# Heads of 64 columns worked by twos on TensorE, in a two-layer block with a second block behind it

## The chip, the cores and the metric

One core of one Trainium2 chip. The metric is the device time of one execution of the whole program in microseconds (us); a figure for a kernel is the median over its runs. A profile is of one execution, which has its own time.

## The reference, cut to what matters

512 tokens of width 1024 go through a first block of two layers and a second block of one. The part that the change touches is attention with heads of 64 columns, in three forms, and the norms:

```python
# first block, per layer: 'a' (8 heads, one shared key and value head, top-k mask)
rel = relu(einsum('thd,sd->ths', qi, ki))              # 4 index heads of 64
iscore = einsum('ths,th->ts', rel, wi); sel = top_k(where(causal, iscore, -inf), 128)
o_a = softmax(mask_sel(qa @ ka.T / 8)) @ va            # 8 heads of 64
# 'b' (4 heads, two score maps each, values of 128 columns)
o_b = (softmax(q1 @ k1.T / 8) - lam * softmax(q2 @ k2.T / 8)) @ vb
h = h + (sigmoid(gate_a) * (o_a @ w_a) + sigmoid(gate_b) * (norm(o_b) @ w_b)) @ w_out
h = h + (gelu(conv(rms_norm(h) @ w_up_gate)) * conv(rms_norm(h) @ w_up_val)) @ w_down
h = h + sigmoid(rms_norm(h) @ w_ple_gate) * (p @ w_ple_proj)
# second block: 'c' (8 heads of 64, own keys and values, bias by distance), a recurrence
# over 8 heads, 32 experts of which each token uses 2, layer norms in place of rms norms
```

## The kernel before, in words

Everything is fp32. Large weights are cut into two rounded parts: ScalarE copies a block to wh (L1805, a "cut"), VectorE subtracts for wl (L1274), and each product is three matmuls (hi x hi, lo x hi, hi x lo; L873 to L875, L1036 to L1038). Weight blocks come by DMA into a ring of three. The activations lie transposed, hT[:, k, :] for k of 8 parts by 512 tokens. All five engines have their program in a fixed order written out by hand; they meet through semaphores, and eight PSUM banks are given out beforehand by a plan (`bank.plan`): `opened(key)` on TensorE waits until the bank's previous use is emptied, `filled` and `emptied` count.

Attention (`attention`, L1061 for TensorE, L1474 for VectorE, ScalarE's likewise) walks a list of jobs; m is 0 and 1 for the two layers (16 jobs "b", then 32 jobs "a") and 2 for the second block (32 jobs "c"). A job is (kind, ti, h): 128 queries ti, head h, keys up to 128(ti+1), outer loop over ti, inner over h. Step s does on TensorE: scores of job s (L1079, banks 2 to 4 in turn); some pieces of a gate projection (`fill` says how many: 4, 2 or 1; L1036 to L1038); the transposes of job s-2's probabilities (L1087, banks 5 and 6); the values of job s-3 (L1109, bank 7, all heads of one ti). Head h has rows 64*(h%2) of the query and key tiles, and its values go to partitions 64*(h%2) of bank 7. VectorE does in step s a cut if one is due (`cuts_at`), then scale, mask and row minimum of job s (L1496), then the normalization of job s-1 (L1541, L1544). ScalarE does the cut, the exponential of job s (L1907), the copy of job s-2's transposed probabilities to PT[(s-2)%2] (L1913), and every fourth step of "a" (second of "b") the sigmoid of a finished gate (L1893). "b" jobs have two score maps (e=0, 1, on rows 0 to 63 and 64 to 127) and their output gets a norm of its own (L898 sums, L905 spread).

The projections (`first_projections`, 21 steps) hold the index scores: twelve (three ti by four heads), two in each of steps 5 to 10, one at the step's start and one after the rotation (L1027, bank 6), all in bank 7 (L958). ScalarE takes the relu of each (L1857), the second one as the last thing of its step, behind the square of the step's tile (L1872). VectorE adds them up and later seeks the top 128 by repeated max8 (L1440, L1443).

A norm (r = 0 to 7) is: squares of the eight parts on ScalarE (L1814), seven additions to ACC on VectorE (L1283, L1290), column sums over ACC on TensorE (L898: 4 matmuls, 8 passes), scaling, root and reciprocal on four columns (L1295, L1818, L1297), a spread back over the partitions (L905), then u and its two rounded parts, one k after the other (L1307, L1822, L1315). Norms 6 and 7 are layer norms and sum hT itself. The FFN's first up tile waits for each k of it; the second up tile follows whole. `spread_heads` (L914) and the recurrence's products (L2262) are not changed; they are matmuls of 64 output columns that lie in the two halves in turn.

## Time and profile before

| | |
|---|---|
| median of 3 runs | 3105.61 us (3098.68 to 3106.81) |
| profiled execution, own time | 3098.97 us |
| its span, mean granted TensorE clock | 3097.5 us, 0.942 |
| TensorE matmul busy | 2842.3 us, 92% |
| VectorE busy | 1674.8 us, 54% |
| ScalarE busy | 1230.0 us, 40% |
| HBM | 110 GB/s over the span |

The profiled execution is 1.5 us longer than its span, and 6.6 us shorter than the median. A matmul's row begins where its first column enters; its end is modelled and reaches over the start of the next, so the distance of two starts is what a matmul costs the engine.

### The profile page before, as it was taken

To read this page: it belongs to the slowest core of one execution; us is meant where nothing else is said; L and a number is where in the kernel's file an instruction comes from. 1 tells how busy PE (TensorE), PEld (TensorE's weight loads), DVE (VectorE), ACT (ScalarE), POOL (GpSimd) and SP (SyncE) were. 2 spreads that over 40 slices of the span, in tenths; PEclk is the share of its full clock that TensorE was granted. 3 is DMA by queue.
4 is the path that set the end of the run, shared out by engine and by line. 5 is a ranking of instruction groups with operands and counts; after the bars stand their busy time and mean duration, and the time that the engine had idled before them with its cause. 6 is when DMAs were issued, how large, how long until landed. Compare 5 with 4: busy or idle time off the path is not lost.

```text
span 3097.5 us, 36057 instructions
## 1 busy us (share of the span) xinstructions
PE 2842.3 (92%) x14676; PEld 2102.9 (68%) x14676; DVE 1674.8 (54%) x2758; ACT 1230.0 (40%) x1793; POOL 119.5 (4%) x101
## 2 busy tenths in 40 slices
PE   6989999999999998999999998998989889679986
PEld 5766677888877776667788875856667658344445
DVE  4596445545445487445646455344433525477767
ACT  2217643423343216642424233244222322267665
POOL 0010000000000010000000000000000000022210
PEclk9999999999999899999999998989989889789998
DMA  3111222222222111223222221302111023379992
GB/s 116 65 55 67 73 106 89 96 95 95 92 85 69 57 69 62 75 80 118 82 95 96 95 82 68 124 24 77 42 44 52 35 90 135 151 260 392 372 347 95
DMA packets 64137, 334.90 MB, mean 108 GB/s; under 512 B 9568, under 2 KB 10336, under 8 KB 31072
## 3 DMA queue, kind: packets, MB, share of 16 engines
q1 hardware_dynamic: 58848, 324.14, 29.0%
q0 software_dynamic: 5120, 8.40, 0.9%
q8 instruction: 118, 1.93, 0.3%
q14 instruction: 51, 0.42, 0.0%
HBM read 312.58 MB, written 28.31 MB: 110 GB/s over the span
## 4 chain that ended last, share of the span: by engine, by line
PE 77%; DVE 12%; ACT 5%; DMA 3%; issue 2%; SPq 0%; POOL 0%; POOLq 0%; DVEq 0%; ACTq 0%
PE bank L873 14%; PE bank L875 14%; PE bank L874 14%; PE bank L1036 3%; PE bank L1079 2%; PE bank L1109 2%; PE bank L1038 2%; PE bank L1037 2%; PE bank L2931 2%; PE bank L2212 2%; ACT wh L1805 1%; DVE wl L1274 1%; PE bank L2917 1%; DMA arena<-in_WE 1%; PE bank L2918 1%
## 5 line engine op out<-in xcount | busy, mean ns | idle before, releaser
L873 PE MATMUL bank<-XH,wh 128*128 128x512 f32 x1344 | 542.8, 404 | 21.0 <-DVE XL L1315 16.9
L874 PE MATMUL bank<-XL,wh 128*128 128x512 f32 x1344 | 531.8, 396 | 0.0
L875 PE MATMUL bank<-XH,wl 128*128 128x512 f32 x1344 | 531.4, 395 | 0.0
L1274 DVE TENSOR_TENSOR wl<-raw,wh 128x2048 fp32r<-128x2048 f32 (+1 forms) x168 | 371.8, 2215 | 225.9 <-ACT wh L1805 225.7
L1805 ACT ACTIVATE wh<-raw 128x2048 fp32r<-128x2048 f32 (+1 forms) x168 | 308.9, 1841 | 189.0 <-DMA raw<-in_W 186.7
L873 PEld LDWEIGHTS bank<-XH,wh 128*128 128x128 f32 x1344 | 257.0, 191 | 105.9 <-issue 26.0
L875 PEld LDWEIGHTS bank<-XH,wl 128*128 128x128 f32 x1344 | 257.4, 192 | 55.4
L874 PEld LDWEIGHTS bank<-XL,wh 128*128 128x128 f32 x1344 | 257.8, 192 | 52.4 <-issue 1.9
L873 PE MATMUL bank<-arena_rounded,wh 128*128 128x512 f32 x576 | 230.5, 400 | 5.3 <-DVE arena_rounded L1519 3.2
L874 PE MATMUL bank<-arena_rounded,wh 128*128 128x512 f32 x576 | 229.0, 398 | 0.0
L875 PE MATMUL bank<-arena_rounded,wl 128*128 128x512 f32 x576 | 228.9, 397 | 0.0
L1036 PE MATMUL bank<-XH,wh 128*128 128x512 f32 (+1 forms) x408 | 193.8, 475 | 0.0
L1616 DVE SCALAR_TENSOR_TENSOR scr<-bank,sml,scr 128x511 f32<-128x511 f32 x88 | 66.0, 750 | 194.0 <-ACT scr L1973 194.0
L1037 PE MATMUL bank<-XL,wh 128*128 128x512 f32 (+1 forms) x408 | 167.7, 411 | 0.0
L1038 PE MATMUL bank<-XH,wl 128*128 128x512 f32 (+1 forms) x408 | 167.3, 410 | 0.0
L1973 ACT ACTIVATE scr<-bank,sml 128x512 f32<-128x512 f32 x88 | 68.6, 780 | 246.2 <-PE bank L875 246.2
L1907 ACT ACTIVATE scr<-scr,tiny 128x128 f32<-128x128 f32 (+3 forms) x160 | 89.3, 559 | 191.3 <-DVE tiny L1496 190.9
L1079 PE MATMUL bank<-arena 64*128 64x128 f32 (+3 forms) x320 | 116.4, 496 | 18.6 <-DVE tiny L1496 18.4
L873 PEld LDWEIGHTS bank<-arena_rounded,wh 128*128 128x128 f32 x576 | 109.8, 191 | 34.5 <-issue 5.2
L1036 PEld LDWEIGHTS bank<-XH,wh 128*128 128x128 f32 (+1 forms) x408 | 80.0, 196 | 76.2 <-issue 58.7
L875 PEld LDWEIGHTS bank<-arena_rounded,wl 128*128 128x128 f32 x576 | 109.5, 190 | 25.9
L874 PEld LDWEIGHTS bank<-arena_rounded,wh 128*128 128x128 f32 x576 | 109.8, 191 | 25.1
(477 smaller groups left out, 4703.6 us busy)
## 6 DMA issues: line engine op xcount, KB each, us to landing
raw<-in_W SPq DMA_DIRECT2D x153, 1024.0 KB, 4.9
arena<-in_WE SPq DMA_DIRECT2D x56, 1024.0 KB
hT<-in_WE SPq DMA_DIRECT2D x26, 1024.0 KB, 10.0
cst<-in_WE SPq DMA_DIRECT2D x14, 1024.0 KB, 9.8
gsave<-scr SPq DMA_DIRECT2D x48, 256.0 KB, 2.4
scr<-gsave SPq DMA_DIRECT2D x48, 256.0 KB, 4.0
raw<-in_W SPq DMA_DIRECT2D x8, 768.0 KB, 4.3
arena<-ytok SPq DMA_DIRECT2D x8, 512.0 KB, 7.1
```

The source lines that it names most:

```text
L873: pe.matmul(ps[0:c.stop - c.start, :], h[:, k, c], hi, start=i == 0, stop=False)
L874: pe.matmul(ps[0:c.stop - c.start, :], h[:, k, c], lo, start=False, stop=False)
L875: mm = pe.matmul(ps[0:c.stop - c.start, :], l[:, k, c], hi, start=False, stop=i == len(xs) - 1)
L1036: pe.matmul(o, h[:, k, c], hi, start=k == 0, stop=False)
L1037: pe.matmul(o, h[:, k, c], lo, start=False, stop=False)
L1038: mm = pe.matmul(o, l[:, k, c], hi, start=False, stop=k == KT - 1)
L1079: mm = pe.matmul(ps[:, 0:wide(ti)], q, k, start=True, stop=True)
L1274: w_lo.inc(dve.tensor_tensor(wl[:, i % 3, 0:k], raw[:, i % 3, 0:k], wh[:, i % 3, 0:k].bitcast(F32), ALU.subtract), i)
L1616: v.inc(dve.scalar_tensor_tensor(out=s[:, 1:T], in0=bank.ap(key)[:, 0:T - 1], scalar=K(f"cw1{li}", f), in1=s[:, 1:T], op0=ALU.mult, op1=AL ...
L1805: w_hi.inc(act.activation(wh[:, i % 3, 0:k], raw[:, i % 3, 0:k], ACT.Copy), i)
L1907: sexp.inc(act.activation(dst[:, 0:n], dst[:, 0:n], ACT.Exp, scale=-1.0, bias=c, accum_out=c_sum), (m, s, e))
L1973: aff.inc(act.activation((FV if which else FG)[q % 2][i], bank.ap(key), ACT.Identity, scale=K(f"cw2{li}", f), bias=K(f"cb{li}", f)), (li, ...
```

## The change

Attention: for "a" and "c" jobs TensorE issues the scores of two heads in one step (every even one), after opening both banks; they lie on rows 0 to 63 and 64 to 127 of the array. The values of two heads are issued together, block by block in turn, so that they lie in the two halves of the output columns; this comes in even steps, for jobs s-4 and s-3, and now stands ahead of the transposes. "b" keeps its values and its place for them; its two score maps are issued after both banks are open. The index scores go by twos at the start of the step, in banks 7 and 6 (bank 6 is shared with the rotation). VectorE's and ScalarE's order in attention and in the projections stays.

Norms: the last addition to ACC is gone from VectorE; TensorE sums ACC (with parts 0 to 6) and then the last square (norms 0 to 5) or the last part of hT (6 and 7) into the same four columns. ScalarE takes a root of a constant ahead of time (`root_table`): at the start of `out_linear`, before the last down tiles of an FFN, and before the last square of `ple`. VectorE's last cut of an FFN moves behind its last addition. The first two up tiles of an FFN are interleaved over k (`two_tiles`), each k waiting for u once. ScalarE waits for the first constants before the layers.

```diff
+                for i in scores_at(s):
+                    bank.plan(("score", li, i), 7 - i % 2)
...
+        def products_at(jobs, s):
+
+            if s >= len(jobs):
+                return ()
+            if jobs[s][0] == "b":
+                return ((s, 0), (s, 1))
+            return ((s, 0), (s + 1, 0)) if jobs[s][2] % 2 == 0 else ()
+
+        def values_at(jobs, s):
+
+            if not 0 <= s - 3 < len(jobs):
+                return ()
+            if jobs[s - 3][0] == "b":
+                return (s - 3,)
+            return (s - 4, s - 3) if jobs[s - 3][2] % 2 else ()
+
         def plan_attention(m):
             jobs = jobs_of(m)
             n_s, n_p, g = 0, 0, 0
             for s in range(len(jobs) + 6):
-                if s < len(jobs):
-                    for e in range(2 if jobs[s][0] == "b" else 1):
-                        bank.plan(("qk", m, s, e), 2 + n_s % 3)
-                        n_s += 1
+                for i, e in products_at(jobs, s):
+                    bank.plan(("qk", m, i, e), 2 + n_s % 3)
+                    n_s += 1
...
-                if 0 <= s - 3 < len(jobs) and jobs[s - 3][2] == 0:
-                    bank.plan(("acc", m, jobs[s - 3][0], jobs[s - 3][1]), 7)
+                if values_at(jobs, s) and jobs[values_at(jobs, s)[0]][2] == 0:
+                    kind, ti, _ = jobs[values_at(jobs, s)[0]]
+                    bank.plan(("acc", m, kind, ti), 7)
...
+            def two_tiles(keys, w, fresh):
+
+                ps = [opened(key) for key in keys]
+                h, l = w
+                for k, hi, lo in xs:
+                    pe.wait_ge(*fresh(k))
+                    for i, key in enumerate(keys):
+                        c = slice(128 * i, 128 * i + 128)
+                        pe.matmul(ps[i], h[:, k, c], hi, start=k == 0, stop=False)
+                        pe.matmul(ps[i], h[:, k, c], lo, start=False, stop=False)
+                        mm = pe.matmul(ps[i], l[:, k, c], hi, start=False, stop=k == KT - 1)
+                        if k == KT - 1:
+                            bank.filled(mm, key)
...
+            def norm_sums(r):
+
+                key = ("sum", r)
+                ps = opened(key)
+                last, ready = (SQ[1], square((r, 7))) if r < 6 else (hT[:, 7, :], h_ready(r, 7))
+                for src, when in ((ACC, added((r, 6))), (last, ready)):
+                    pe.wait_ge(*when)
+                    for ti in range(4):
+                        mm = pe.matmul(ps[:, ti:ti + 1], src[:, tt(ti)], ones[:, 0:1], start=src is ACC and ti == 0,
+                                       stop=src is not ACC, skip_group_check=True)
+                bank.filled(mm, key)
+
             def rms(r, between=None):
-                column_sums(("sum", r), ACC, ones[:, 0:1], added((r, 7)))
+                norm_sums(r)
...
-                def score(i):
-                    ti, h = score_of(i)
-                    ps = opened(("score", li, i))
-                    if i == 0:
+                def two_scores(pair):
+                    ps = [opened(("score", li, i)) for i in pair]
+                    if pair[0] == 0:
                         for t in range(3):
                             pe.wait_ge(*roped(li, t))
-                    r0 = 64 * (h % 2)
-                    mm = pe.matmul(ps[:, 0:wide(ti)], A_(QI + 512 * (h // 2), 512)[r0:r0 + 64, tt(ti)],
-                                   A_(KI, 512)[r0:r0 + 64, 0:wide(ti)], start=True, stop=True)
-                    bank.filled(mm, ("score", li, i))
+                    for out, i in zip(ps, pair):
+                        ti, h = score_of(i)
+                        r0 = 64 * (h % 2)
+                        mm = pe.matmul(out[:, 0:wide(ti)], A_(QI + 512 * (h // 2), 512)[r0:r0 + 64, tt(ti)],
+                                       A_(KI, 512)[r0:r0 + 64, 0:wide(ti)], start=True, stop=True)
+                        bank.filled(mm, ("score", li, i))
 
                 for s in range(21):
-                    for i in scores_at(s)[0:1]:
-                        score(i)
+                    if scores_at(s):
+                        two_scores(scores_at(s))
...
-                    if s < len(todo):
+                    pair = products_at(todo, s)
+                    if pair:
                         kind, ti, h = todo[s]
-                        for e in range(2 if kind == "b" else 1):
-                            ps = opened(("qk", m, s, e))
-                            if kind == "b" and s < 4:
-                                pe.wait_ge(*roped(m, 4 + h))
-                                pe.wait_ge(*roped(m, 8 + h))
-                            if kind == "a" and ti == 0:
-                                pe.wait_ge(*roped(m, 12 + h // 2))
-                                pe.wait_ge(*roped(m, 3))
-                            if kind == "c" and ti == 0:
-                                pe.wait_ge(*bank.empty(("q2", h // 2)))
-                                pe.wait_ge(*bank.empty(("k2", h // 2)))
-                            q, k, _ = qk_of(m, s, e)
-                            mm = pe.matmul(ps[:, 0:wide(ti)], q, k, start=True, stop=True)
-                            bank.filled(mm, ("qk", m, s, e))
+                        ps = [opened(("qk", m, i, e)) for i, e in pair]
+                        if kind == "b" and s < 4:
+                            pe.wait_ge(*roped(m, 4 + h))
+                            pe.wait_ge(*roped(m, 8 + h))
+                        if kind == "a" and ti == 0:
+                            pe.wait_ge(*roped(m, 12 + h // 2))
+                            pe.wait_ge(*roped(m, 3))
+                        if kind == "c" and ti == 0:
+                            pe.wait_ge(*bank.empty(("q2", h // 2)))
+                            pe.wait_ge(*bank.empty(("k2", h // 2)))
+                        for out, (i, e) in zip(ps, pair):
+                            q, k, _ = qk_of(m, i, e)
+                            mm = pe.matmul(out[:, 0:wide(ti)], q, k, start=True, stop=True)
+                            bank.filled(mm, ("qk", m, i, e))
                     for _ in range(fill(m, s)):
...
+                    done = values_at(todo, s)
+                    if len(done) == 2:
+                        kind, ti, h = todo[done[0]]
+                        key = ("acc", m, kind, ti)
+                        if h == 0:
+                            opened(key)
+                        for i in done:
+                            pe.wait_ge(*bank.empty(("turn", m, i)))
+                        if s == 4 and m == 2:
+                            for t8 in range(8):
+                                pe.wait_ge(*bank.empty(("v2", t8)))
+                        for j in range(ti + 1):
+                            for i in done:
+                                h = todo[i][2]
+                                r0 = 64 * (h % 2)
+                                v_ = wv[:, j, 0:64] if kind == "a" else vn[:, j, 64 * h:64 * h + 64]
+                                mm = pe.matmul(bank.ap(key)[r0:r0 + 64, tt(h // 2)], v_, PT[i % 2][:, tt(j)],
+                                               start=j == 0, stop=j == ti)
+                        if h == 7:
+                            bank.filled(mm, key)
...
-                    if 0 <= s - 3 < len(todo):
+                    if len(done) == 1:
...
+                            if q == 0 and which == 0:
+                                two_tiles([("up", li, 0, 0, i) for i in range(2)], weights(n, 256), lambda k: x((3 * li + 1, k)))
+                            else:
+                                for i in range(2):
+                                    tile(("up", li, q, which, i), weights(n, 256), slice(128 * i, 128 * i + 128), xs)
...
                     for k in range(8):
-                        if k % 2:
+                        last = ci == 2 and k == 7
+                        if k % 2 and not last:
                             cuts_to(n + 2)
-                            n += 1
                         key = ("down", li, ci, k)
                         dve.wait_ge(*bank.full(key))
                         bank.emptied(dve.tensor_tensor(hT[:, k, :], bank.ap(key), hT[:, k, :], ALU.add), key)
                         if ci == 2 and k >= 2:
                             add_to_norm(3 * li + 2, k - 1)
-                add_to_norm(3 * li + 2, 7)
+                        if last:
+                            cuts_to(n + 2)
+                        n += k % 2
...
+            def root_table():
+
+                act.activation(tz(204), ones[:, 0:1], ACT.Sqrt)
...
```

The same lines, not shown: `layer_norm` calls `norm_sums`; `added` has an event less for each norm; `add_to_norm(r, 7)` is gone from `out_linear` and `ple`, and from the start of VectorE's program.

## Rows read from the trace of the kernel before

**Rows 1.** The page: busy time of each engine, and the chain that ended last.
```profile
PE 2842.3 (92%) x14676; PEld 2102.9 (68%) x14676; DVE 1674.8 (54%) x2758; ACT 1230.0 (40%) x1793; POOL 119.5 (4%) x101
...
PE 77%; DVE 12%; ACT 5%; DMA 3%; issue 2%; SPq 0%; POOL 0%; POOLq 0%; DVEq 0%; ACTq 0%
```

**Rows 2.** Stretches: length, busy PE, PEld, DVE, ACT, POOL, PEclk, DMA share, GB/s.
```profile
322.00:427.00 105.00, 98.91 (x448) 64.59 (x447) 43.39 (x129) 62.90 (x118) 0.00 (x0) 0.97 0.14 49
...
2013.00:2104.00 91.00, 88.25 (x385) 52.11 (x383) 36.76 (x125) 42.82 (x104) 0.00 (x0) 0.91 0.08 27
```

**Rows 3.** Timeline of PE, "a" steps: start us, us, what, count.
```profile
344.03 0.43 PE L1109 MATMUL bank<-scr,arena 128*64 128x128 f32 x2
344.39 0.70 PE L1079 MATMUL bank<-arena 64*128 64x256 f32 x2
...
413.39 0.60 PE L1087 MATMUL bank<-cst,scr 128*128 128x128 f32 x4
413.92 1.09 PE L1109 MATMUL bank<-scr,arena 128*64 128x128 f32 x8
414.93 1.12 PE L1079 MATMUL bank<-arena 64*128 64x512 f32 x2
415.99 0.50 PE L1036 MATMUL bank<-XH,wh 128*128 128x512 f32 x1
...
417.50 0.27 PE L1087 MATMUL bank<-cst,scr 128*128 128x128 f32 x1
```

**Rows 4.** Timeline of PE, both score maps of a "b" job.
```profile
303.82 1.13 PE L1079 MATMUL bank<-arena 64*128 64x512 f32 x4
```

**Rows 5.** Chain in order of time: start us, us to the next, what.
```profile
2233.21 3.69 PE bank L2262 x64
...
2370.17 1.39 PE bank L914 x16
```

**Rows 6.** Timeline at a weight cut of the second block; idle before in brackets.
```profile
2033.69 1.90 ACT L1805 ACTIVATE wh<-raw 128x2048 fp32r<-128x2048 f32 x1
...
2035.63 2.29 DVE L1274 TENSOR_TENSOR wl<-raw,wh 128x2048 fp32r<-128x2048 f32 x1 [2.92 <-ACT wh L1805]
...
2038.87 0.41 PE L1087 MATMUL bank<-cst,scr 128*128 128x128 f32 x2 [2.04 <-DVE scr L1544]
```

**Rows 7.** Timeline of ACT at a gate, where "b" ends.
```profile
326.81 1.28 ACT L1893 ACT_TABLE_LOAD   x1
...
328.10 0.60 ACT L1893 ACTIVATE scr<-bank 128x512 f32<-128x512 f32 x1
```

**Rows 8.** Timeline, second index score of a pair and the next.
```profile
109.86 0.91 PE L958 MATMUL bank<-arena 64*128 64x384 f32 x2
...
110.81 0.49 ACT L1857 ACTIVATE scr<-bank 128x384 f32<-128x384 f32 x1 [1.03 <-PE bank L958]
...
111.35 0.91 PE L958 MATMUL bank<-arena 64*128 64x384 f32 x2 [0.58 <-ACT scr L1857]
```

**Rows 9.** Timeline of PE, first up tile of layer 0.
```profile
530.71 0.63 PE L874 MATMUL bank<-XL,wh 128*128 128x512 f32 x1
531.13 0.63 PE L875 MATMUL bank<-XH,wl 128*128 128x512 f32 x1
...
537.62 0.50 PE L873 MATMUL bank<-XH,wh 128*128 128x512 f32 x1 [0.30 <-DVE XL L1315]
```

**Rows 10.** Timeline around the sums of norms 1 and 2.
```profile
522.03 1.48 DVE L1283 TENSOR_TENSOR scr<-scr 128x512 f32<-128x512 f32 x2
...
522.80 1.28 ACT L1818 ACT_TABLE_LOAD   x1
...
523.66 1.32 PE L898 MATMUL bank<-cst,scr 128*128 128x1 f32 x8 [2.27 <-DVE scr L1283]
...
896.53 2.29 DVE L1274 TENSOR_TENSOR wl<-raw,wh 128x2048 fp32r<-128x2048 f32 x1 [1.90 <-ACT wh L1805]
...
900.97 1.84 PE L898 MATMUL bank<-cst,scr 128*128 128x1 f32 x8 [3.48 <-DVE scr L1283]
```

More of the change, by code:

```diff
@@ L313, in plan_win @@
                     bank.plan(("rot", li, t), 6)
-                for i in scores_at(s):
-                    bank.plan(("score", li, i), 7)
         def scores_at(s):
@@ L544, in program @@
         square = Signal(sem("square"), [(r, k) for r in rms_at for k in range(8)])
-        added = Signal(sem("added"), [(r, k) for r in ALLN for k in range(1, 8)])
+        added = Signal(sem("added"), [(r, k) for r in ALLN for k in range(1, 7)])
         nroot = Signal(sem("nroot"), ALLN)
@@ L926, in layer_norm @@
             def layer_norm(r):
-                column_sums(("sum", r), ACC, ones[:, 0:1], added((r, 7)))
+                norm_sums(r)
                 spread(("mean", r), normcols(r), bank.empty(("sum", r)))
@@ L1009, in first_projections @@
                         rotate(li, t)
-                    for i in scores_at(s)[1:2]:
-                        score(i)
                     if t is not None:
@@ L1093, in attention @@
                             opened(key)
[L1094 removed]
                         pe.wait_ge(*bank.empty(("turn", m, s - 3)))
[L1096 removed]
+                        if s == 3:
                             for t8 in range(8):
                                 pe.wait_ge(*bank.empty(("vb", m, t8)))
[L1099 to L1101 removed]
                         for j in range(ti + 1):
[L1103 to L1110 removed]
+                            mm = pe.matmul(bank.ap(key)[:, tt(h)], vb[:, j, tt(h)], PT[(s - 3) % 2][:, tt(j)],
+                                           start=j == 0, stop=j == ti)
+                        if h == 3:
                             bank.filled(mm, key)
@@ L1139, in ffn @@
                             split(n)
-                            for i in range(2):
-                                first = q == 0 and which == 0 and i == 0
-                                tile(("up", li, q, which, i), weights(n, 256), slice(128 * i, 128 * i + 128), xs,
-                                     (lambda k: x((3 * li + 1, k))) if first else None)
+                            if q == 0 and which == 0:
[3 more added lines that the diff above has]
+                                    tile(("up", li, q, which, i), weights(n, 256), slice(128 * i, 128 * i + 128), xs)
                             n += 1
@@ L1660, in ple @@
                         add_to_norm(r, k - 1)
-                add_to_norm(r, 7)
             cuts_to(0)
             dve.wait_ge(s_in, 16)
-            for k in range(1, 8):
+            for k in range(1, 7):
                 add_to_norm(0, k)
@@ L2002, in ple @@
                         square_of(r, k - 1)
+                root_table()
                 square_of(r, 7)
```

18 lines of the change are left out of this document (4 added, 14 removed).

## The prediction

> **What bounds the kernel now.** I read the page first, then the chain of waits, then the stretches in which 64-column heads are worked, then single steps. TensorE is busy 92% of the span and is 77% of the chain that ended last [rows 1]; VectorE and ScalarE have half or more of their time free. In the attention stretches (layer 0's "a" heads 322 to 427 us, the second block's "c" heads 2013 to 2104; layer 1 repeats layer 0) TensorE is busy 99 of 105 and 88 of 91 us, ScalarE 63 and 43 [rows 2]. So there TensorE's own time is the price, and what it sheds comes off the end unless a wait takes its place.
>
> One step at ti=3 shows where its time lies [rows 3]. From the first transpose at 413.39 to the next at 417.50 it takes 4.11 us: transposes to 413.92 (0.53), values (L1109) to 414.93 (1.01), scores (L1079) to 415.99 (1.06), gate pieces to 417.50 (1.51). Each fp32 matmul is two passes. The eight value passes start over 0.82 us, 0.05 of it the first weight load, so about 0.109 apart. The last one's own 0.109 ends at 414.84 and the scores start at 414.93: 0.09 passes empty whenever the shape of the tile changes, three times in a step. Values of one block (344.03 to 344.39) take 0.36, so a block adds 0.22. Scores of 256 columns span 0.70 against 1.12 for 512, so a block of 128 adds 0.21.
>
> **The change, part by part.**
> (1) *Pairs in attention.* Three runs of 32 jobs (a, a, c; eight heads at each ti) become 16 pairs each. Is a pair as cheap as one head? For scores, branch "b" already does it: four passes, two heads on different row halves and banks, span 1.13 us, where two passes of one head span 1.12 [rows 4]. For values, the nearest rows are L2262, whose 64 passes of 128 columns (full height, output halves changing every second matmul, other data in each half) take 3.69 us, 0.058 each, and L914, which changes halves at every matmul as the new loop does: 16 in 1.39, part of it at half clock [rows 5]. At the lone head's 0.109 these would be 7.0 and 1.74. I take one pair for the price of one head. The lower bound of the gain is none at all for values (rival 2). The Trainium skill speaks against halves by column (page "TensorE: Matmul & The Clock Gate", Part 3, "The mechanism"): a weight load overlaps a running matmul only when the row group differs, and both heads of a value pair use all rows. By that rule values would cost what they do now and the sum would be 36; by L914 it is 62.
>
> Per pair goes one value group, one score group, and of the six changes of tile shape in two steps two (0.09 each, with a first weight load of 0.05 to 0.11 standing open behind each). At ti=3 two steps now cost 8.22. After: scores 1.06, gates 1.51 + 0.09, values 1.01, transposes 0.49, gates of the odd step 1.40, transposes 0.53, together 6.09. Gain 2.13. With 0.22 and 0.21 less per block: 1.7, 1.26, 0.82 at ti = 2, 1, 0. Four pairs of each: 23.6 per run, **70.7 us** for three.
>
> What is lost of it. (a) Weight cuts. At 2033.69 ScalarE cuts a block (1.90), VectorE waits and subtracts (2.29), and only then comes to the reduce that the transpose at 2038.87 needs: 5.2 us that no faster TensorE shortens, and it idles 2.04 [rows 6]. With about 1 us less work beneath each cut the idle grows: 3.6 for the second block's three cuts (+0.7, +1.0, and at the third, where two longer steps just cover it now, +1.9); for layers 0 and 1 three each, +0.6, +0.8, +0.3. (b) The hole behind 326.8, where the end of branch "b" waits for ScalarE's table loads with a sigmoid and a root between them, not for TensorE [rows 7]: the four short steps before it save 0.4 each in vain, 1.6 per layer. (c) Each gate (every fourth step) keeps ScalarE for two table loads and a sigmoid, 1.28 x 2 + 0.60 = 3.2 us [rows 7]. At ti=1 a step becomes 0.6 us shorter. My walk through the queues leaves 0.1 to 1 us of slack at a gate, so I put 1.5 per layer. Lost: 3.6 + 2 x (1.7 + 1.6 + 1.5) = 13.2. Remains **57.5**.
>
> Order: values move ahead of the transposes, so that PT[s%2] is read before ScalarE may overwrite it; the wait for the copy of turn s-3 is covered by scores and gates (2.3 us or more against a copy of 0.3 to 0.6). Queued behind that wait are only the transposes. "b" jobs: opening both banks first holds e=0 back until e=1's bank is free, but VectorE frees that bank before it comes to e=0 anyway: 0.
>
> (2) *Index scores.* Twelve single groups a layer become six pairs: on paper 0.6 to 1.2 per pair. But bank 6 is also the rotation's, and the second relu stays at the end of ScalarE's step. Before, the second of a pair starts at 109.86, its relu is at 110.81, and the next step's score waits until 111.35 (idle 0.58) [rows 8]. After, TensorE comes to the pair at 109.86 and waits for the relu, which now only has to follow the square of the tile just finished: pair at about 110.4, next tile about 0.9 sooner. In the steps with a rotation (6, 9, 10) the rotation waits for the relu, 0.5 to 0.7, and gives back what the pairing saves; at steps 5 and 8 a copy or a root is ahead of the relu. I count 1.8 a layer, and half of it kept, since VectorE (top-k) is full at the end of the projections: **2** in all (bounds 0 and 8).
>
> (3) *First two up tiles interleaved.* Before, tile 0 keeps pace with VectorE's u (1.26 a row); it starts at 530.1 and runs at 0.42 a matmul (half clock, so TensorE was full anyway) and 0.23 later, and the last row starts at 537.62 [rows 9]; then 2 + 24 matmuls make 544.0. Interleaved, 48 matmuls from 530.1, about ten at 0.43, the rest at 0.23, end at 543.1. **2** for two layers. If the clock rises earlier, 4; if later, 0.
>
> (4) *Norm sums.* VectorE's last add (0.70) goes and eight passes come. The sum over ACC cannot start before add 6 ends (522.71), when square 7 is nearly ready, so 16 passes follow instead of 0.70 and 8. Eight take 1.32 at mixed clock, 1.84 at half [rows 10]: norms 1, 4, 7 lose 0.2 to 0.5, norms 3 and 6 0.7 to 0.9: together 2.5 worse. Norm 0 ends on a weight cut as before. The early root table: its load at 522.80 already runs while TensorE sums (523.66 on), so 0; before norms 3 and 6 it delays square 7 by 0.6, hidden behind the first eight passes. The cut moved behind the last add of the FFN: wl stood from 896.53 to 898.82 before the last add, though TensorE was done at 897.49 (900.97 less its idle 3.48) [rows 10]. That gives about 1.3 net at norms 2 and 5: 2.6. Sum **0**, and **0.5** for less time at half clock behind them.
>
> Sum: 57.5 + 2 + 2 + 0.5 = 62. The profiled execution took 3098.97 us: 3037. The median of the three runs is 6.6 above it (their spread is 8), so I add half: **3040**.
>
> **The rivals.**
> 1. *ScalarE takes over.* For: a burst of 3.2 us every fourth step, with steps a quarter shorter. Against: ScalarE is busy 63 of 105, VectorE 43 [rows 2], and would stay under 80%. Price: 1.2 us at each of 16 gates, 19: gain 43, 3059. The Trainium skill has this rival as a rule (page "TensorEngine Tiling (Array Packing)", "PSUM Bottleneck"): packing speeds TensorE but not the emptying of its banks.
> 2. *Value halves do not run side by side* (loads stand open). For: the lone head shows nothing of it. Against: L914. Price: the 480 value passes keep their 0.109; half of 52 us, 26, is not saved: gain 36, 3066.
> 3. *Fewer losses.* Odd jobs have their scores a step earlier, so cuts and gates cost nothing new (13), and norms 2 and 5 stay at full clock (4): gain 79, 3023.
> 4. *Slower: the clock.* After the idle of 2.04 us at 2036.8 TensorE ran at 1.2 GHz; the clock missing in that stretch (0.09 of 91 us) is 8 us lost. If the new idles did this, seven such drops eat most of the 62 us and the eighth makes it slower; the stretches hold nine cuts, so nearly every one would have to bring one. For: the second block's stretch has 0.91 of the clock [rows 2]. Against: layer 0's has 0.97 though it holds the idle of 3 us in the hole. 3110.
>
> That pairing does nothing at all is excluded for scores by rows 4.
>
> **How the numbers follow.** Forecast 0.55 (its own range 3028 to 3052: losses 1 to 25 instead of 13), rival 1 0.20, rival 2 0.12, rival 3 0.08, rival 4 0.05. Predicted is the likeliest, 3040. The range takes in all but the fourth with a little for run to run: 3018 to 3068. 0.3% of 3105.6 is 9.3 us, which is about what this kernel's measurement can tell. Only rival 4 reaches there: faster 0.93, same 0.03, slower 0.04.
>
> **What would show it.** Right: value passes of a pair 0.055 apart; L1079's successor with x4 groups of the same span as x2 now; steps of ti=3 in twos near 6.1 us; a stretch of about 87 instead of 105. Idle before transposes behind cuts, released by VectorE, near 3 us at the second block's. Part 2: rotations waiting for relus. Part 4: x16 sum groups. Wrong: value passes still 0.109 apart, idle spread over all gate steps, or half clock in stretches now at full.

## The result, and the profile after

The changed kernel takes 3056.17 us (median of 4 runs, 3046.29 to 3057.62), the kernel before 3103.76 on the same chip: a ratio of 0.9846, 95% interval 0.983 to 0.9863. That is 47.6 us, where 62 (the sum) to 66 (3105.6 less 3040) were forecast. The profiled executions are 41.4 us apart (3098.97 and 3057.62).

The page of the changed kernel, busy times and the chain that ended last, beside [rows 1]:

```profile
PE 2773.1 (91%) x14740; PEld 2077.3 (68%) x14740; DVE 1666.7 (55%) x2750; ACT 1227.2 (40%) x1800; POOL 119.3 (4%) x101
...
PE 77%; DVE 11%; ACT 5%; DMA 4%; issue 3%; SPq 0%; POOL 0%; POOLq 0%; DVEq 0%; ACTq 0%
```

TensorE shed 69 us of busy time and the span only 41: the rest is new idle. Steps first. Below, a "turn" is what the transposes make of a job's probabilities, and ScalarE's copy of a turn (L1971) is what the values read. This is the timeline at ti=3 (start us, us, what, count), the answer to [rows 3]:

```profile
409.88 0.60 PE L1149 MATMUL bank<-cst,scr 128*128 128x128 f32 x4
410.41 1.13 PE L1121 MATMUL bank<-arena 64*128 64x512 f32 x4
411.47 0.50 PE L1077 MATMUL bank<-XH,wh 128*128 128x512 f32 x1
...
413.06 1.09 PE L1141 MATMUL bank<-scr,arena 128*64 128x128 f32 x16
414.08 0.66 PE L1149 MATMUL bank<-cst,scr 128*128 128x128 f32 x4
...
415.97 0.60 PE L1149 MATMUL bank<-cst,scr 128*128 128x128 f32 x4
```

From 409.88 to 415.97 two steps take 6.09 us, the number of the prediction. Both heads' scores span 1.13 (L1121, x4), both heads' values 1.09 (L1141, x16): sixteen passes in the time of eight. So the arithmetic of a pair was right. What was wrong stands between the pairs. A weight cut in layer 0, steps 35 and 36, from the timeline of all engines:

```profile
372.26 1.91 ACT L1859 ACTIVATE wh<-raw 128x2048 fp32r<-128x2048 f32 x1
...
374.21 2.29 DVE L1328 TENSOR_TENSOR wl<-raw,wh 128x2048 fp32r<-128x2048 f32 x1 [1.10 <-ACT wh L1859]
...
376.42 0.61 DVE L1550 CUSTOM_DVE_ANT_0 scr<-bank,arena,tiny 128x384 f32<-128x384 f32 x1
...
377.07 0.61 ACT L1965 ACTIVATE scr<-scr,tiny 128x384 f32<-128x384 f32 x1 [2.90 <-DVE tiny L1550]
...
377.69 0.47 ACT L1971 ACTIVATE scr<-bank 128x384 f32<-128x384 f32 x1
...
378.30 1.55 PE L1141 MATMUL bank<-scr,arena 128*64 128x128 f32 x12 [2.80 <-ACT scr L1971]
```

Read upwards: the value pair waits 2.80 us for ScalarE's copy of turn 33 (L1971). That copy was ready to be made long before, but stands in ScalarE's queue behind exp 35, which waits for VectorE's reduce (L1550), which stands behind VectorE's subtraction (L1328), which waited for ScalarE's cut (L1859). The other two cuts of the stretch idle TensorE 2.65 and 2.92 us in the same way, and the second block's 2.03, 4.07 and 1.49, with 1.17 behind the gate that follows the last. Before, these six were 0.54, 0.00, 0.00 and 0.71, 2.04, 0.00, with 0.99 and 0.68 behind the gates that follow the first two. The waits of the stretch 322 to 417 (total us, times, longest) name one releaser for the three cuts and for 2.05 us where branch "b" ends:

```profile
PE bank L1141 <- ACT scr L1971: 10.4, 4, 2.9
```

And the stretches (columns as in [rows 2]); the second one is what follows the idle at 378.30:

```profile
322.00:417.00 95.00, 81.20 (x453) 56.17 (x452) 42.59 (x129) 63.10 (x121) 0.00 (x0) 0.93 0.15 53
378.00:382.00 4.00, 3.70 (x20) 3.12 (x21) 1.13 (x6) 3.94 (x7) 0.00 (x0) 0.57 0.17 66
1987.00:2057.70 70.70, 61.12 (x383) 37.07 (x381) 35.55 (x124) 42.06 (x103) 0.00 (x0) 0.95 0.10 36
```

The third, the "c" heads, has 70.7 us where it had 91, though TensorE stands idle for 9.6 of them. The granted clock of layer 0's stretch fell from 0.97 to 0.93: behind 2.80 us without work TensorE goes on at 1.2 GHz for a while (the group of L1141 above spans 1.55 us, where twelve passes at full clock span 0.88). A stretch at 1.2 GHz counts 0.5 in the mean, so the mean over the whole run says how long it ran at the lower level, half of which is lost: (1 - 0.935) x 2 x 3056 = 397 us, against (1 - 0.942) x 2 x 3097 = 359 before.

Where the 41 us came from, by marks in both traces: "a" heads 12.4 and 11.5 us in layers 0 and 1 (18.8 each forecast), "c" heads 20.0 (20.0), all else together -2.7 of the 41.2 us of span (4.5).

### The profile page after: what moved, and what is told of

The parts are those of the page before. It is cut to its first block, busy times and chain, and to the rows that moved or that the text cites. A ratio compares the mean times of both kernels' runs of the same rounds, so it can differ in the third digit from the quotient of the medians.

```text
span 3056.3 us, 36284 instructions
## 1 busy us (share of the span) xinstructions
PE 2773.1 (91%) x14740; PEld 2077.3 (68%) x14740; DVE 1666.7 (55%) x2750; ACT 1227.2 (40%) x1800; POOL 119.3 (4%) x101
## 4 chain that ended last, share of the span: by engine, by line
PE 77%; DVE 11%; ACT 5%; DMA 4%; issue 3%; SPq 0%; POOL 0%; POOLq 0%; DVEq 0%; ACTq 0%
PE bank L889 14%; PE bank L891 14%; PE bank L890 14%; PE bank L1077 3%; DMA arena<-in_WE 2%; PE bank L1078 2%; PE bank L1079 2%; PE bank L2275 2%; ACT wh L1859 1%; DVE wl L1328 1%; PE bank L1121 1%; PE bank L2994 1%; PE bank L2980 1%; PE bank L1149 1%; PE bank L2981 1%
## 5 line engine op out<-in xcount | busy, mean ns | idle before, releaser
L889 PE MATMUL bank<-XH,wh 128*128 128x512 f32 x1312 | 528.4, 403 | 14.0 <-DVE XL L1369 10.1
L890 PE MATMUL bank<-XL,wh 128*128 128x512 f32 x1312 | 518.0, 395 | 0.0
L891 PE MATMUL bank<-XH,wl 128*128 128x512 f32 x1312 | 517.7, 395 | 0.0
L1328 DVE TENSOR_TENSOR wl<-raw,wh 128x2048 fp32r<-128x2048 f32 (+1 forms) x168 | 371.8, 2215 | 222.0 <-ACT wh L1859 221.9
L1859 ACT ACTIVATE wh<-raw 128x2048 fp32r<-128x2048 f32 (+1 forms) x168 | 309.0, 1841 | 191.2 <-DMA raw<-in_W 189.1
L889 PEld LDWEIGHTS bank<-XH,wh 128*128 128x128 f32 x1312 | 250.2, 191 | 91.4 <-issue 20.2
L891 PEld LDWEIGHTS bank<-XH,wl 128*128 128x128 f32 x1312 | 250.5, 191 | 53.5
L890 PEld LDWEIGHTS bank<-XL,wh 128*128 128x128 f32 x1312 | 251.1, 191 | 51.9 <-issue 2.4
L1876 ACT ACTIVATE XH<-scr 128x512 fp32r<-128x512 f32 x72 | 45.2, 631 | 158.8 <-DVE scr L1631 112.9
## 6 DMA issues: line engine op xcount, KB each, us to landing
arena<-in_WE SPq DMA_DIRECT2D x56, 1024.0 KB, 10.4
```

Source lines behind the costliest of these rows:

```text
L889: pe.matmul(ps[0:c.stop - c.start, :], h[:, k, c], hi, start=i == 0, stop=False)
L890: pe.matmul(ps[0:c.stop - c.start, :], h[:, k, c], lo, start=False, stop=False)
L891: mm = pe.matmul(ps[0:c.stop - c.start, :], l[:, k, c], hi, start=False, stop=i == len(xs) - 1)
L1328: w_lo.inc(dve.tensor_tensor(wl[:, i % 3, 0:k], raw[:, i % 3, 0:k], wh[:, i % 3, 0:k].bitcast(F32), ALU.subtract), i)
L1859: w_hi.inc(act.activation(wh[:, i % 3, 0:k], raw[:, i % 3, 0:k], ACT.Copy), i)
```

## The experiments

All times below are medians, ratios against the kernel before on the same chip. Except where said, each is the changed kernel with the one edit. They ran on several chips, on which the kernel before has medians of 3099.8 to 3103.9, so a difference of two runs is good to some 4 us at best.

**One: is it a matter of which step holds the cut?** Pairs are worked in even steps, and the cuts stood in odd ones.

```
 (both engines' attention)
-                    for n in cuts_at(m, s):
+                    for n in cuts_at(m, s - 1):
```

> The changed kernel with the weight cuts that lie between attention steps made one step later on both engines (steps 28, 36, 44 in place of 27, 35, 43 in a layer's a heads; 4, 12, 24 in place of 3, 11, 23 in the second block). Nothing else is changed. Theory P (phase): a value pair is worked in even steps only and needs the copy of the odd turn before it, which ScalarE makes in the odd step behind its cut and its exp; so a cut in an odd step stops TensorE by 2.7 to 2.9 us and one in an even step does not, since the copies made there are needed two steps later. VectorE still subtracts behind the same cut, so an idle of about 1 us before transposes stays at some cuts. Expected 12 to 22 us faster than the changed kernel. Theory V (VectorE): what TensorE waits for is the reduce behind VectorE's 2.3 us, whichever step it lies in: idles of 2 us and more stay, now before transposes, and the time is within 5 us of the changed kernel.

3060.01 us, ratio 0.9862 (0.9845 to 0.988): no gain at all. Its timeline, a cut in step 36:

```profile
374.53 1.91 ACT L1859 ACTIVATE wh<-raw 128x2048 fp32r<-128x2048 f32 x1
...
376.47 2.29 DVE L1328 TENSOR_TENSOR wl<-raw,wh 128x2048 fp32r<-128x2048 f32 x1 [4.33 <-ACT wh L1859]
...
379.97 0.87 PE L1149 MATMUL bank<-cst,scr 128*128 128x128 f32 x3 [3.79 <-DVE scr L1598]
```

The values no longer wait, as theory P had it, but the transposes do, a step later and for 3.79 us, because VectorE's normalization (L1598) stands behind the same subtraction. Theory P falls. Theory V is right here.

**Two: ScalarE and VectorE cut in different steps** (ScalarE `s - 1`, VectorE `s - 2`).

> As the run before, with VectorE's subtraction one step later still (ScalarE cuts in step 28, VectorE subtracts in step 29), so that VectorE doesn't stand 1.9 us waiting for ScalarE's half with a reduce queued behind it. By theory P the last of the idle at cuts goes (under 0.5 us at each of the nine), 3 to 10 us faster than the run with both one step later, 18 to 28 us faster than the changed kernel. By theory V this is the run that gains, all at once, and the run before gained nothing. If TensorE's clock falls only behind these idles, its time at half speed also goes back by some 20 us.

3012.54 us, ratio 0.9714 (0.9698 to 0.973): 43.6 us faster than the changed kernel, more than the 18 to 28 that were forecast. The clock rose to 0.943. VectorE still comes to its subtraction before ScalarE's half is done, but the reduce and the normalization of the step between are now ahead of it. Of the idle, 1.5 to 2.2 us are left at most cuts, in the step behind VectorE's, before values again.

**Three: ScalarE's copy ahead of its exp**, in cut steps alone, cuts where they were.

```
+                    def exps():
...
+                    def copy():
...
+                    for act_of in ((copy, exps) if cuts_at(m, s) else (exps, copy)):
+                        act_of()
```

> The changed kernel, but in the steps that hold a weight cut ScalarE makes its copy of the turn ahead of its exp (everywhere else behind it, as now). Theory P: the value pair behind the cut starts at once, the transposes after it still wait about 1 us for VectorE's normalization; idle per cut 2.8 goes to about 1.0, in all 8 to 16 us faster than the changed kernel. Theory V: the idle moves as a whole from the values to the transposes, 2.3 us or more remain, less than 4 us faster.

3039.35 us (3020.86 to 3040.50), ratio 0.9783 (0.9751 to 0.9816), 16.8 faster by medians, a little over theory P's 8 to 16. In the timeline the values start unhindered and the transposes wait:

```profile
372.61 0.88 PE L1141 MATMUL bank<-scr,arena 128*64 128x128 f32 x12
...
374.90 0.52 PE L1149 MATMUL bank<-cst,scr 128*128 128x128 f32 x3 [1.41 <-DVE scr L1598]
```

Behind them the next values wait another 0.8 us. Theory V, which had under 4 us, falls with this one. Each of them held for one of the two queues: a cut blocks both, and TensorE waits for the later.

**Four: the order of a value pair's matmuls.**

```
-                        for j in range(ti + 1):
-                            for i in done:
+                        for i in done:
+                            for j in range(ti + 1):
```

> The changed kernel with the two loops over a value pair exchanged: all blocks of one head, then all blocks of the other, so that the column halves of the array change once in a pair and not at every matmul. If two halves run side by side only when they are issued alternately, the 480 value passes go back from about 0.055 to 0.109 us each and the time rises by 20 to 26 us. If the order doesn't matter (the array takes up the other half's work from further on), it stays within 4 us.

3053.43 us, ratio 0.9847 (0.983 to 0.9863), the same as changed. A group of sixteen passes grows from 1.09 us to 1.58, where sixteen in a row at a lone head's 0.109 would be 1.96 (15 starts, 0.05 for the first load, 0.27 for the last pass):

```profile
412.88 1.58 PE L1141 MATMUL bank<-scr,arena 128*64 128x128 f32 x16
```

In the records the second head's first pass starts 0.49 us after the first head's first, while the first head's last passes are still to start; from there the two go side by side. The three stretches together are about 3 us longer, which other stretches hid. So halves of columns overlap even when they are not issued alternately, only less. Neither forecast (20 to 26, none) was quite it.

**Five: VectorE's cut one step later again** (ScalarE `s - 1`, VectorE `s - 3`).

> The changed kernel, ScalarE's weight cuts one attention step later and VectorE's three later (a cut at steps 28 and 30, where the run with cuts spread has 28 and 29). In the spread run TensorE still idles 1.5 to 2.1 us once a cut, in the even step behind VectorE's (30, 38, 46), before values, whose copy of the odd turn stands in ScalarE's queue behind an exp that waits for a reduce behind VectorE's subtraction. Theory C (the chain copy behind exp behind reduce behind subtraction): with VectorE's part in an even step that copy is the even turn's, which is wanted two steps later, so these idles fall under 0.5 us and it is 8 to 15 us faster than the spread run (about 3000). Theory V (any step is too short for 2.3 us of VectorE): the idle moves one step on to the transposes of step 31, 1 to 2 us, no faster than the spread run by more than 3 us.

2999.71 us, ratio 0.967 (0.965 to 0.9689), 12.8 faster than two. Theory C holds in the second block, where the idle behind the second cut fell from 1.52 to nothing and 0.38 came a step on. In the "a" heads 0.9 to 1.1 us stay, and the timeline shows another burst as their cause, on ScalarE:

```profile
362.15 1.28 ACT L1951 ACT_TABLE_LOAD   x1
...
363.44 0.60 ACT L1951 ACTIVATE scr<-bank 128x512 f32<-128x512 f32 x1
...
363.93 1.91 ACT L1859 ACTIVATE wh<-raw 128x2048 fp32r<-128x2048 f32 x1
...
365.86 1.28 ACT L1965 ACT_TABLE_LOAD   x1
```

A gate, the cut and the table load for the next exp: 5 us in a row.

**Six: the copy first in every step**, with the cuts of five.

> As the run with the wider cuts, and ScalarE makes its copy of a turn ahead of the exp in every step of 64-column heads, not behind it. Theory C: the copy is then never behind VectorE's work, and the last idles before values are gone; where the wider cuts have removed them already, within 3 us of that run. The rival: the exp now waits for the transposes of the same step, which TensorE makes last in it; if the loop transposes, copy, exp, normalization is longer than two steps anywhere (short steps at ti=0 and 1), idles of 0.3 to 1 us appear before transposes in many steps and it is 5 to 20 us slower than that run.

3012.48 us, ratio 0.9712 (0.9693 to 0.9731), 12.8 slower than five. The rival holds: idles of 0.6 to 1.2 us in steps 23, 31, 39 and 47, which had 0 to 0.5 in run five, and 0.2 to 1.1 in steps 9, 15 and 27 of the second block. What heals a cut step harms the others.

**Seven: the kernel before with the cuts of two.**

> The kernel before, unpaired, with its cuts in attention placed as in the spread run (ScalarE one step later, VectorE two). The spread placement took 44 us off the changed kernel. If what it removed there are idles that the shorter steps of pairs have opened, the kernel before, which idles only 0.5 to 3.0 us at some of these cuts (in layers 0 and 1 together some 12 us, 2.8 in the second block), gains 5 to 15 us from it, and pairs are worth 75 us or more once the cuts stand so. If the placement is a gain of its own that has nothing to do with pairs, it gains 30 us or more.

3072.84 us, ratio 0.9913 (0.9893 to 0.9932): 27.0 us faster than before, between the two answers and nearer the upper one. So the placement is a gain of its own; pairs add to it. Against run two pairs and the rest are worth 60.3 us here, not 75.

**Eight: index scores one by one again.**

```
-                    if scores_at(s):
-                        two_scores(scores_at(s))
+                    for i in scores_at(s)[0:1]:
+                        score(i)
```
(and the second behind the rotation, both in bank 7)

> The changed kernel with the index scores one by one again (one at the head of a step and one behind the rotation, both in bank 7), all else as changed. My prediction put the pairs at a gain of 2 us (bounds 0 and 8): then this run is 2 us slower than the changed kernel. In the trace of the changed kernel the stretch from the first index score to the first turn takes 0.7 us less in layer 0 and 5.6 less in layer 1 than before, though both do the same work: if the 5.6 is owed to the pairs, 5 to 7 us slower; if it is run to run, within 3 us.

3063.37 us (3057.52 to 3066.83), ratio 0.9878 (0.9859 to 0.9897), 7.2 slower than the changed kernel by medians (whose runs reach 3057.6) and 10 by ratios. The index pairs are worth more than my 2, near my upper bound of 8 or over it. In the two profiled executions the stretch from the first index score to the first turn takes 7.3 us more than with pairs in layer 0 and 3.9 more in layer 1; but in the other runs with pairs the same stretch varies by some 5 us, so this is a size and not a figure. The wait that I forecast is there in the changed kernel, 0.37 us where I had put about 0.5 (the last column of L1001); the rotations wait 0.17 to 0.39 us for a relu, less than the 0.5 to 0.7 forecast:

```profile
112.69 0.48 ACT L1915 ACTIVATE scr<-bank 128x384 f32<-128x384 f32 x1
...
113.32 0.92 PE L1001 MATMUL bank<-arena 64*128 64x384 f32 x4 [0.37 <-ACT scr L1915]
```

**Nine: the cuts kept away from the gates too.** "b" heads one (ScalarE) and two (VectorE) steps later, "a" heads three and five, second block one and three.

```
+        def cuts_late(m, s, d_b, d_a):
+            if m == 2:
+                return cuts_at(m, s - (1 if d_b == 1 else 3))
+            return (cuts_at(m, s - d_b) if s - d_b < 16 else []) + (cuts_at(m, s - d_a) if s - d_a >= 16 else [])
...
-                    for n in cuts_at(m, s):
+                    for n in cuts_late(m, s, 1, 3):
```
(ScalarE; VectorE has `cuts_late(m, s, 2, 5)`)

> The changed kernel with the cuts placed by what the earlier runs showed. In a layer's a heads the trace of the wider cuts has 0.9 to 1.1 us idle at each cut step because ScalarE's cut (1.9 us) directly follows a gate (table load 1.28, sigmoid 0.60) and is followed by the next table load (1.28); so ScalarE's cut moves two more steps on, away from the gate (steps 30, 38, 46), and VectorE's to 32, 40, 48. In the b heads the closer placement (ScalarE one later, VectorE two) comes back, since the wider one left 1.8 us idle at step 17; the second block keeps one and three. If the burst on ScalarE is the cause, the idles at 30, 38 and 46 go and it is 6 to 12 us faster than the wider cuts, near 2992. If the cuts cost about 1 us wherever they stand, it is within 3 us of them.

2991.34 us, ratio 0.9626 (0.9603 to 0.9648): the fastest of all, 64.8 us below the changed kernel and 111 below the one before. The idles of the "a" heads beside the cut (0.9 to 1.1 us in run five) are gone, so the burst was their cause. The 8.4 us against run five are not all theirs, since the cuts of the "b" heads moved back in the same run. The stretches that answer to the ones above, with the granted clock at 1.00:

```profile
319.00:393.00 74.00, 72.20 (x440) 49.06 (x439) 41.42 (x124) 59.88 (x117) 0.00 (x0) 1.00 0.22 78
1932.00:1993.00 61.00, 58.81 (x384) 35.85 (x382) 34.93 (x121) 41.71 (x103) 0.00 (x0) 1.00 0.13 44
```

and the same cut as above, with no idle in any row of PE about it:

```profile
361.98 1.91 ACT L1864 ACTIVATE wh<-raw 128x2048 fp32r<-128x2048 f32 x1
...
362.95 0.88 PE L1146 MATMUL bank<-scr,arena 128*64 128x128 f32 x12
363.76 0.55 PE L1154 MATMUL bank<-cst,scr 128*128 128x128 f32 x3
...
365.05 2.29 DVE L1333 TENSOR_TENSOR wl<-raw,wh 128x2048 fp32r<-128x2048 f32 x1
...
365.52 0.49 PE L1154 MATMUL bank<-cst,scr 128*128 128x128 f32 x3
365.94 1.13 PE L1126 MATMUL bank<-arena 64*128 64x512 f32 x4
```

**Ten: norms as before** (sum of one tensor in eight passes behind VectorE's seventh add, no early table load, the FFN's last cut ahead of the last add).

> The changed kernel with its norms as in the kernel before: VectorE makes the last of the seven adds and TensorE sums one tensor in eight passes, no early load of the root's table, and the last weight cut of the FFN ahead of VectorE's last add. Pairs everywhere as changed. I had put this part at 0, made of 2.5 lost at norms 1, 3, 4, 6, 7 and 2.6 won at norms 2 and 5. By the trace of the changed kernel norms 1, 3, 4 and 7 cost 0.7 to 1.8 us each (5.3 in all, twice my sum), while the stretches from norm 1 to 2 and from 4 to 5 end 4.2 and 2.2 us earlier. If both readings belong to this part it is about 0 to 3 us slower than the changed kernel; if the gain of those stretches comes from the up tiles instead, it is 2 to 5 us faster.

3059.48 us (3049.06 to 3060.15), ratio 0.9846 (0.9825 to 0.9866): 3.3 slower by medians, and the ranges overlap. The part is worth 0 to 3 us. A norm of the changed kernel:

```profile
514.16 1.92 PE L956 MATMUL bank<-cst,scr 128*128 128x1 f32 x16 [1.47 <-DVE scr L1337]
```

Sixteen passes take 1.92 us where eight took 1.32 [rows 10]; but from the last turn to the end of norm 1's sums it is 95.6 us before, 96.9 in the changed kernel and 96.8 with the old norms, so what I read as their cost is mostly not theirs. From norm 1's spread to norm 2's the changed kernel is 4.2 us shorter than the one before, and 1.4 with the old norms. That leaves 2.7 for the moved cut (I had 1.3) and 1.4 for the up tiles (I had 1). Between norms 4 and 5 it is 2.2 and 0.8.

**Eleven: the kernel before with the cuts of nine.**

> The kernel before, unpaired, with its cuts in attention placed as in the run with the cuts apart (b heads one and two steps later, a heads three and five, second block one and three). Together with that run it gives what the whole change is worth where no cut stops TensorE on either side. My gross sum for the pairs in attention was 70.7 us, less 3.2 for the hole behind branch b, plus 4.5 for the other parts: 72. If that sum is right this kernel is near 2991 + 72 = 3063, some 10 us faster than the one before with cuts spread (3073). If the sum was too large by the 10 us that the changed kernel fell short of it, it is near 3053.

3062.51 us (3061.75 to 3072.95), ratio 0.988 (0.9859 to 0.99), to 3063 forecast. The whole change is worth 3062.5 - 2991.3 = 71.2 us here. The ratios of the two runs say 79 (0.0254 of 3103), for one of this kernel's four runs took 3072.95; so this figure is good to some 8 us. The same stretches of this kernel:

```profile
326.00:419.00 93.00, 93.00 (x440) 61.31 (x440) 41.63 (x121) 61.59 (x114) 0.00 (x0) 1.00 0.17 60
1989.00:2070.00 81.00, 81.00 (x390) 49.23 (x389) 36.55 (x124) 43.38 (x104) 0.00 (x0) 1.00 0.10 35
```

No cut stops TensorE in the "a" heads now, nor in this kernel's "c" heads. But one still does in branch "b", once in each layer, where VectorE has the end of its top-k work and then the subtraction ahead of the reduce: 3.23 us in this kernel and 4.02 in run nine. And run nine has 0.38 and 0.90 us left behind cuts of the "c" heads. The rows, first of this kernel, then of run nine:

```profile
247.22 1.22 PE L1084 MATMUL bank<-arena 64*128 64x256 f32 x2 [3.23 <-DVE tiny L1501]
...
243.55 1.23 PE L1126 MATMUL bank<-arena 64*128 64x256 f32 x4 [4.02 <-DVE tiny L1555]
```

**Twelve: pairs of scores alone**, on top of nine; values go one head at a time behind the transposes.

> The run with the cuts apart, in which the values of 64-column heads are again worked one head at a time, each step its own, behind the transposes; scores stay in pairs. It says what part of the gain the value halves carry. By the prediction's rows a lone value group spans 0.36, 0.58, 0.79 and 1.01 us at ti = 0 to 3, twelve pairs of each in all: 33 us slower than the run with the cuts apart (near 3024). If the halves run side by side only in part, 10 to 25 us slower. If the pair's values had cost more through their place ahead of the transposes (their wait for the copy), under 10.

3018.15 us (3011.83 to 3019.1), ratio 0.9721 (0.9704 to 0.9737): 26.8 slower than nine, where 33 were forecast. The value pairs carry some four tenths of the gain, and the prediction's price for losing them (rival 2) was 26.

| stretch, us | before | changed | before, cuts apart | changed, cuts apart |
|---|---|---|---|---|
| "a" heads, layer 0 | 98.8 | 86.3 | 93.2 | 72.7 |
| "a" heads, layer 1 | 98.2 | 86.7 | 93.2 | 72.7 |
| "c" heads | 90.7 | 70.6 | 79.9 | 60.5 |
| kernel (median) | 3103.8 | 3056.2 | 3062.5 | 2991.3 |

(From the start of branch "b"'s last spread, or the block's first turn, to the last turn.)

## Why the gain fell short by a quarter

**The gross gain was right as a sum, and in part by luck.** I had 70.7 for the pairs, 3.2 of it lost in the hole, 4.5 for the rest: 72.0. Runs nine and eleven give 71.2. But stretch by stretch they give 20.5, 20.6 and 19.4 us, against 23.6 a run less 1.6 for the hole in layers 0 and 1: with what came through at the hole 63.0, where I had 67.5. The rest of the change is worth about 8, where I had 4.5, and the two errors cancel. Two steps of "c" heads at ti=3 went from 6.81 to 4.70 us, 2.11 saved to 2.13 forecast; at ti=2, 1, 0 1.66, 1.13, 0.84 to 1.7, 1.26, 0.82. So the steps themselves are as forecast. What is missing is in part idle that run nine has and run eleven has not: ahead of the last two turns the pair of values waits 0.78 us in the "a" heads and 0.83 in the "c" heads for a copy, which I had not counted, and two cuts of the "c" heads leave 0.38 and 0.90.

**The step that failed is (a), the weight cuts**, put at 7.0 us in all. The medians give what moving the cuts takes away: 3103.8 - 3062.5 = 41.3 us in the kernel before, 3056.2 - 2991.3 = 64.8 in the changed one. So the change made them 23.6 us dearer, which is by arithmetic what separates 71.2 from 47.6. By the table 17 of it lie in the "a" heads (5.6 and 5.0 us a layer before, 13.6 and 14.0 in the changed kernel), and from the first turn to the last spread of "b" the same marks give 3.4 (7.8 and 6.3, then 10.2 and 7.3). The "c" heads give nothing (10.8, then 10.1); some 4 us are not located.

TensorE's idle in all three attention stretches (first to last turn) was 24 us before and 54 in the changed kernel; with the cuts apart 8 and 15. I see four mistakes in my term; only the second has a run of its own.

- I took the idle to grow by the work that went from beneath one cut (0.3 to 1.9 us), where it grew by 1.1 to 2.9, the idle behind the next gate counted in.
- I wrote that the wait for the copy of turn s-3 is covered "by scores and gates (2.3 us or more against a copy of 0.3 to 0.6)": I set the cover against the copy's length, and not against what stands ahead of the copy in ScalarE's queue, the exp that waits for VectorE. Run three, which takes away only that order, wins 16.8 us.
- I counted the cuts of "a" and "c" heads alone, but in branch "b" TensorE idles 9.0 us in layer 0 of the changed kernel, 5.3 before. Not all of that need be the cuts: "b" now opens both banks before its first score, a term that I put at 0, and with the cuts apart 5.1 us against 3.2 remain. No run takes this term away alone.
- The price of an idle is not its length. At step 44 of layer 0 2.92 us of idle lengthened the step by 3.87 and the next by 0.7, because the clock was at 1.2 GHz behind it.

**The "c" heads came out at 20.0 by two errors that cancel.** I had 23.6 less 3.6 for the cuts. With the cuts apart the pairs bring 19.4, and the cuts cost no more than before (10.1 us to 10.8). Their idles at cuts grew by 6.0 us, not 3.6, but the clock, at 0.51 for 17 us behind the second cut in the kernel before (2040 to 2057), was back much sooner in the changed kernel, at 0.54 only from 2010 to 2017. The rival on the clock, at 0.05, was right in kind for layers 0 and 1 and had the wrong sign for this one.

**(b), the hole**, 1.6 us lost per layer: the loss is there, but for another reason than the one I gave. Of its 3.0 us the changed kernel keeps 2.94, and its step before it idles 2.05 (0.80 before). I had given the table loads all of it. Run eleven moves the cuts alone, and of the 3.04 us 0.28 are left; in runs two and nine 0.65. So it was mostly the cut in step 19. With the cuts apart 1.2 of the 1.6 come through in each layer.

**(c), gates on ScalarE**, 3.0 us, and rival 1 with 19: nothing. In steps that hold a gate and no cut the changed kernel has no idle, and neither has run nine in its "a" heads, with ScalarE busy 59.88 of 74 us. A gate hurts only next to a cut (run five; 1.17 us in the changed kernel's "c" heads, 0.90 in run nine's, and 0.99 and 0.68 in layer 0 of the kernel before). The Trainium skill (page "TensorEngine Tiling (Array Packing)", "PSUM Bottleneck") says that emptying the banks may become the limit once TensorE is four times faster. At two heads side by side it is not: TensorE waits for such a copy for 0.78 us in the 74 of run nine, and the 10.4 us of the changed kernel are owed to what stood ahead of the copy, not to the copy.

**Rival 2, value halves one after the other:** refuted by the 1.09 us of sixteen passes and by runs four and twelve. The Trainium skill's rule (page "TensorE: Matmul & The Clock Gate", Part 3, "The mechanism") that a weight load overlaps a running matmul only across row groups does not hold in these rows: passes with all 128 rows and different column halves go two per 0.109 us. The measurement decides.

**Rival 3, fewer losses**, at 0.08: right for the gates, wrong for the cuts. The scores of odd jobs do come a step earlier, but it is the copy and the normalization that stand behind a cut. It also had norms 2 and 5 at full clock, and the stretch around norm 2's sums (884 to 896 us of the changed kernel) has 0.86.

**Parts 2 to 4**, 4.5 us in all: runs nine and eleven leave about 8 for them (71.2 less the 63.0 above), by medians. Index scores are the mis-sized one (about 7 to my 2). Norms were 0 as forecast, within 3, though the moved cut brings 2.7 and 1.4 us where I had 1.3 each.

## What to carry to other kernels

Before a bottleneck engine is made faster, list what the other engines do in one piece (here 1.9 us on ScalarE, then 2.29 on VectorE, the second waiting for the first) and what stands behind it in both queues: a wait's cover is to be set against the whole queue ahead of its releaser, not against the releaser. A long operation in two halves on two engines should not be called in the same step of both; moving them some steps apart, away from other bursts, cost one expression here and won more (64.8 us) than the change had with the cuts where they stood (47.6). Look at what such idle costs already before the change: moving the cuts in the kernel before took away 16 us of idle in attention and 41 us of time, the rest being in part clock ((1 - 0.946) x 2 x 3060 = 330 us at the lower level, 29 less than before, which is worth 14).

## What the runs showed of the hardware

- Matmuls on different column halves of the array, each on all rows, overlap fully when alternated (0.0545 us a pass against 0.109) and in part when issued one half's after the other's. Two heads at ti=3 took 1.09 us alternated and 1.58 in turn; at a lone head's pace they would take 1.96, an estimate from its 0.109.
- What an idle does to the clock didn't go by its length alone. 2.04 us in the kernel before (2036.8) was followed by 17 us at 0.51, some 8 us of work; 2.03 us at the second block's first cut in the changed kernel lengthened its step by 2.1 and cost no more; 4.07 us at its second cut cost 6.7 in all. In layer 0 of the changed kernel 2.65 us was followed by no fall of the clock, 2.80 and 2.92 by 3.4 us at the lower level each. Why is open: no run here sets the work ahead of an idle apart from its length.
